# The residual's load and norm put ahead of the memory's in the setup of a two-layer decoder step

## The reference, cut to what matters

```
D_MODEL = 1024
def rms_norm(x, gain):
    x32 = x.astype(jnp.float32)
    y = x32 * lax.rsqrt(jnp.mean(x32 * x32, axis=-1, keepdims=True) + EPS)
    return (y * gain.astype(jnp.float32)).astype(x.dtype)
...
def mem_kv(mem, gain, w_kv, k_gain):
    B, M, _ = mem.shape
    m = rms_norm(mem, gain) @ w_kv
    k = rms_norm(m[..., :MEM_WIDTH].reshape(B, M, MEM_HEADS, MEM_HEAD_DIM), k_gain)
    v = m[..., MEM_WIDTH:].reshape(B, M, MEM_HEADS, MEM_HEAD_DIM)
    return k, v
...
    for i in range(DEPTH):
        hp = rms_norm(xp, norm_mix[i])
        hs = rms_norm(xs, norm_mix[i])
        mkp, mvp = mem_kv(mem_prompt, norm_mem[i], w_mem_kv[i], mem_k_norm[i])
```

## Time and profile before

| what | value |
|---|---|
| median of 3 runs | 3214.2 us (3213.38 to 3219.34) |
| the profiled execution's own time | 3221.07 us |
| its span, first to last instruction | 3219.5 us |
| PE busy in the span | 2985.7 us (93%) |
| DVE, ACT, POOL busy | 1720.0, 1066.8, 93.3 us |
| mean granted TensorE clock | 0.965 of full |

### The profile page before, as it was taken

How to read it: one execution, slowest core, us unless ns; L and a number is a source line. 1 busy time by engine, 2 the same in 40 slices (tenths; PEclk the granted TensorE clock), 3 DMA queues, 4 the chain that set the end, 5 groups by cost and what they waited for, 6 DMA issues and landing times.

```text
span 3219.5 us, 56294 instructions
## 1 busy us (share of the span) xinstructions
PE 2985.7 (93%) x22600; PEld 2691.1 (84%) x22600; DVE 1720.0 (53%) x2527; ACT 1066.8 (33%) x1809; POOL 93.3 (3%) x161
## 2 busy tenths in 40 slices
PE   6996799999999999899975888888999999999997
PEld 6995699999999999799964656556999999999996
DVE  4116224666666666630132666666236666666666
ACT  5223314222222222422233666666032222222221
POOL 0010000000000000000000000000000000000000
PEclk8998899999999999899987999999999999999998
DMA  3122111111111111222316656656301111111101
GB/s 134 51 97 79 64 40 33 40 39 44 54 39 39 39 40 58 81 80 81 101 47 218 229 207 217 206 199 217 110 27 40 43 55 39 39 39 42 56 26 67
DMA packets 190524, 270.05 MB, mean 84 GB/s; under 512 B 9672, under 2 KB 138334, under 8 KB 190396
## 3 DMA queue, kind: packets, MB, share of 16 engines
q1 hardware_dynamic: 171984, 201.68, 18.9%
q0 software_dynamic: 17632, 66.17, 6.3%
q10 hardware_dynamic: 780, 0.34, 0.0%
HBM read 242.70 MB, written 32.14 MB: 85 GB/s over the span
## 4 chain that ended last, share of the span: by engine, by line
PE 82%; DVE 8%; ACT 5%; DMA 2%; issue 1%; ACTq 0%; SPq 0%; POOL 0%; DVEq 0%; POOLq 0%
PE ps L329 23%; PE ps L330 23%; PE ps L331 23%; PE ps L438 2%; PE ps L1146 2%; DVE left L1404 2%; PE ps L1074 1%; DVE x L1953 1%; PE ps L1172 1%; ACT bp_s L1284 1%; PE ps L1086 1%; PE ps L1118 1%; PE ps L1154 1%; DVE bp_s L1406 1%; DMA pk_raw<-in_cache_sb_k_dram 1%
## 5 line engine op out<-in xcount | busy, mean ns | idle before, releaser
L329 PE MATMUL ps<-act_hi,w_hi 128*128 128x370 f32 x2112 | 702.3, 333 | 1.4 <-DVE act_lo L473 1.4
L1953 DVE TENSOR_TENSOR x<-x,ps 128x512 f32<-128x512 f32 (+1 forms) x792 | 538.9, 687 | 305.6 <-PE ps L331 304.7
L330 PE MATMUL ps<-act_lo,w_hi 128*128 128x370 f32 x2112 | 701.6, 332 | 0.0
L331 PE MATMUL ps<-act_hi,w_lo 128*128 128x370 f32 x2112 | 699.7, 331 | 0.0
L329 PE MATMUL ps<-w_hi,act_hi 128*128 128x256 f32 (+1 forms) x1800 | 507.0, 282 | 5.9 <-DVE w_lo L325 1.8
L330 PE MATMUL ps<-w_lo,act_hi 128*128 128x256 f32 (+1 forms) x1800 | 506.3, 281 | 0.0
L331 PE MATMUL ps<-w_hi,act_lo 128*128 128x256 f32 (+1 forms) x1800 | 504.8, 280 | 0.0
L329 PEld LDWEIGHTS ps<-act_hi,w_hi 128*128 128x128 f32 x2112 | 398.7, 189 | 5.7 <-DVE act_lo L473 1.7
L330 PEld LDWEIGHTS ps<-act_lo,w_hi 128*128 128x128 f32 x2112 | 398.4, 189 | 2.0
L331 PEld LDWEIGHTS ps<-act_hi,w_lo 128*128 128x128 f32 x2112 | 398.0, 188 | 0.0
L325 DVE TENSOR_TENSOR w_lo<-w_raw,w_hi 128x2048 fp32r<-128x2048 f32 x73 | 167.3, 2292 | 350.7 <-ACT w_hi L321 350.7
(11 more groups left out here) (285 smaller groups left out, 3568.6 us busy)
## 6 DMA issues: line engine op xcount, KB each, us to landing
pk_raw<-in_cache_sb_k_dram SPq DMA_DIRECT2D x128, 384.0 KB, 3.7
w_raw<-in_w_up_dram SPq DMA_DIRECT2D x88, 512.0 KB, 4.7
d_raw<-in_w_down_dram POOLq DMA_DIRECT2D x44, 512.0 KB, 3.8
projected<-stage POOLq DMA_DIRECT2D x13, 1024.0 KB, 5.2
pv_hi<-in_cache_sb_v_dram SPq DMA_DIRECT2D x32, 384.0 KB, 4.2
pv_lo<-in_cache_sb_v_dram SPq DMA_DIRECT2D x32, 384.0 KB, 4.1
pv_raw<-in_cache_sb_v_dram SPq DMA_DIRECT2D x32, 384.0 KB, 4.3
pv_own<-in_cache_sb_v_dram SPq DMA_DIRECT2D x32, 384.0 KB, 4.4
```

Of the source, the lines that this page charges most:

```text
L329: pe.matmul(out, ahi, bhi, start=first, stop=False, **kw)
L330: pe.matmul(out, ahi, blo, start=False, stop=False, **kw)
L331: return pe.matmul(out, alo, bhi, start=False, stop=last, **kw)
L1953: dve.tensor_tensor(xs, xs, ps[0:ROWS[t], DN_BANK[(2 * t + c) % 4], :], ALU.add).then_inc(dn_ev, 1)
```

## The change

Four of the engine programs are reordered. SP issues x's three transfers first, without the wait on the nine small loads, and the memory's load after them. ScalarE, VectorE and TensorE do the norm of x first, then the memory's norm, and ScalarE and VectorE make the parts of unit 0 after that. In layer 1 the order of the calls on each engine stays as it was. No instruction is added or removed but for the wait.

```
         def _(sp):
-            load_mem(sp)
-
-            sp.wait_ge(set_ld, 16 * 9)
             for g in range(2):
                 sp.dma_start(x[:, 4 * g:4 * g + 4, :], ...).then_inc(x_ld[g], 16)
             sp.dma_start(x[0:NS, NPT, :], ...).then_inc(x_ld[2], 16)
+            load_mem(sp)
...
             for l in (0, 1):
+                act_norm_x(act, c, 8 * l, False, lambda e, t: x_ready(e, t, l, False))
+                act_mem(act, c, l)
                 if l == 0:
-                    act_mem(act, c, l)
                     split_hi(act, 0, 0)
-                act_norm_x(act, c, 8 * l, False, lambda e, t: x_ready(e, t, l, False))
-                if l:
-                    act_mem(act, c, l)
                 act_kv(act, c, l)
...
             for l in (0, 1):
-                if l == 0:
-                    dve_mem(dve, c, l)
-                    split_lo(dve, 0, 0)
                 dve_norm_x(dve, c, 8 * l, False)
                 if l:
                     dve_tails(dve, 0)
-                    dve_mem(dve, c, l)
+                dve_mem(dve, c, l)
+                if l == 0:
+                    split_lo(dve, 0, 0)
                 dve_kv(dve, c, l)
...
-                if l == 0:
-                    pe_mem(pe, c, l)
-                else:
+                if l:
                     pe.wait_ge(dn_ev, DC + 18 * NFT)
                 pe_norm_x(pe, c)
                 if l:
                     pe_tails(pe, 0)
-                    pe_mem(pe, c, l)
+                pe_mem(pe, c, l)
                 pe_kv(pe, c, l)
```

## The result

The changed kernel took 3227.05 us in the median (3216.54 to 3233.56, 16 runs), the kernel before beside it 3213.79 (3208.13 to 3223.39, 16 runs): a ratio of 1.0035 (95% interval 1.0025 to 1.0046), by which it is 11 us slower (the two medians alone differ by 13.3). Two repetitions gave 1.0029 (1.0017 to 1.0041) and 1.0025 (1.0012 to 1.0038), so 8 to 11 us. Executions more than 1.5% above the fastest of the same kernel are left out of all ratios and, where that is said, of medians. The forecast was +5.0 us, with a range up to 3224.0: the direction was right, the size was not.

A forecast was written before the change was run, and what follows sets the result against it. TensorE was taken to bound the kernel from the input projection on, the weight chain to set its start; +4.1 for the weight chain and +0.9 for the clock gave +5.0 us, 3214.2 to 3219.2 us, range 3213.5 to 3224.0.

The forecast's parts named there:

- The weight chain: Weight units' issue, landing, high and low part, 9.19 us a turn; unit 1 ready at 63.64 against 59.58, 4.1 later.
- x's landing: At the kernel's start, x's first transfer was to land at 9.94 us, with bounds of 9.04 and 11.5.
- the table loads: Two ScalarE table loads of 1.28 us each, formerly under the memory's norm, were to lie on the setup's path.
- the memory's norm: In the setup after the norm of x, no longer under x's loads, it was to add 10.28 us.
- The rival of the drain: Each ScalarE table load in the setup drains the engine first: +7.4 us, 3221.6 in total; chance 0.03.
- The norm of x: In the setup, ScalarE was said to pace it, so it kept its old 27.44 us.
- the small loads may land as late as 18.1 and cost nothing: Setup slack: ScalarE's turns of x begin at 24, less 5.9 us taken from the memory's first turn.
- if the setup products wait past 18: Sign of being wrong: TensorE's setup products, which wait for the small loads, wait past 18 us.
- The starving rival: Small loads in the setup land only near 23, beside SP's 6.5 MB stream: +9.9 us, 3224.1; chance 0.07.
- The clock at the projection: TensorE may start the input projection at its low level: 0 to 1.9 us, taken as 0.9.
- the rival of the clock: Low clock past 6 us at the projection's start costs over 2.3 us; at 8 us, +7.5, 3221.7; chance 0.06.
- a later start there is a later end of the same size: From the input projection's first product on, the end follows TensorE, busy for 2985.7 of 3219.5 us.

The follow-up runs named there:

- e3: Changed kernel with weight unit 0 split ahead of the memory's norm: 3215.05 us, ratio 0.9993 to the kernel before; cut behind the input projection, 266.5 us.
- e2: The changed kernel run a second time, nothing edited: 3227.02 us, ratio 1.0029 to the kernel before.
- e18: The changed kernel run a third time, nothing edited: 3224.06 us, ratio 1.0025 to the kernel before.
- the cut kernels: Both kernels ended behind layer 0's input projection, later work left out: before 268.23 us, changed 275.34 and, on another chip, 272.99 us.
- the pair cut at 500 us: Both kernels ended behind layer 0's output projection, later work left out: before 499.18 us, changed 507.33 us in the medians of all six executions.

## Why the prediction was wrong

**The weight chain: right.** One more turn of the weight chain on the path decides. Its turns took 62.22 - 52.96 = 9.26 and 71.56 - 62.22 = 9.34 us against 9.19, and e3 takes the loss back by moving one step off it.

**x's landing, the table loads, the memory's norm: right within 0.6 us.** x landed at 9.38, 9.30 and 9.56 for 9.94, and the memory's norm took 51.13 - 41.31 = 9.82 for 10.28 (10.42 in e2). The accumulator read ends at 15.55, the load begins at 15.56 and the root at 16.86, so the drain that the Trainium skill, "ScalarE: Activation LUTs", section "What ACT_TABLE_LOAD costs", adds isn't there in this trace either. The rival of the drain falls.

**The norm of x: the step that failed.** It stood in the sum at the old 27.44 us. From x's landing and both table loads to the memory's squares it took 41.31 - 9.38 - 2.56 = 29.37, 31.17 in e2 and 29.02 in e18: 1.6 to 3.7 us more. Two sentences led there. "From 27.91 to 55.35 ScalarE paces the norm of x" is a misreading: from 40.97 to 51.97 TensorE paced it, with four turns made ahead under the squares, so the 27.44 held only with that head start. And "the small loads may land as late as 18.1 and cost nothing": they landed at 18.6 to 18.9, just past that line, as the prediction's own sign of being wrong has it ("if the setup products wait past 18"). The line itself was drawn with the memory's first turn; x's turns take twice the products, and four of them at TensorE's low level, 15 products in 3 us, last 6.4 us. An estimate from these rows: with 21.78 - 18.83 = 2.95 us from landing to first turn, the loads would have to land by about 24 - 6.4 - 2.95 = 14.65 for the old head start. The starving rival had the right mechanism and got 0.07, because the mean of the earlier trace rows hid how little the small loads moved while the memory's load ran.

**The clock at the projection: between its bounds.** 0.9 was taken from 0 to 1.9. The first profile paid nothing (fourth tile 9.27 us after unit 2 is ready, as before), e2 8.02 - 7.43 = 0.6, and e18 6.72 - 4.82 = 1.9 (the fifth tile's delay less that of unit 2, which is ready at 73.89 + 2.30 = 76.19 in e2 and at 73.58 in e18, against 68.76). In e18 TensorE stays low from 73.62 to about 79.7, the 6 us at which the rival of the clock began.

**The sum.** The setup costs 4.8 to 7.1 us in the medians of the cut kernels instead of 5.0, so the norm of x alone would have left the time inside the range. The whole kernels differ by 8 to 11, and what is left over, some 1 to 6 us, took it out. The prediction had nothing there, since "a later start there is a later end of the same size"; whether that sentence fails stays open. One by one the lower ends of the three intervals, 8.0, 5.5 and 3.9 us, leave room for hardly any remainder, but weighted by their widths the three give 9.7 us (7.5 to 11.9, an estimate). The plain delay of 7.3 us cost 6.8 (3 to 11), the pair cut at 500 us tells nothing, and where the rest arises was not found. So the norm of x is the one step shown to have failed, and it explains only a part of the miss; the cause of the rest stays open. e3 has no such remainder (1.7 us under before when cut, some 2 as a whole), so what it shares with the changed kernel, the order of the loads and the late turns of x, is not the likely source, though its interval (6 us under to 2 over) leaves some room. The range also took some 2 us for a median's spread from three runs; sixteen runs of one kernel spread over 15 to 17 us.

## What to carry to other kernels

Before a wait is taken out of a load queue, ask who shares the DMA engines with what it held back: here a queue of small packets, while a stream of large ones ran in full, moved at most about a packet for a packet, thus few bytes, and held up an engine that had been early. When a step moves out from under a load, look one link further, at the buffer that it frees: here the first weight unit's split, moved behind a norm, took away the time in which the second unit had been loading. A stretch in which TensorE runs at its low level is free only while another engine covers it, and a stage's old duration is carried over only with the head start that it had.

## What the runs showed of the hardware

0.34 MB in 780 small packets took until 18.6 to 18.9 us beside SP's stream in three executions of the changed kernel and until 8.65 beside 1 MB of it; from 9 to 14 us they got 0.16 MB in 357 packets to SP's 1.61 MB in 394. The granted clock's row isn't to be trusted ahead of the first change in an execution: it says 1.00 at 22 to 25 us while the products run at the pace of 0.50. And at which moment TensorE's level rises within the same work differs between executions by some 3 us (products at the high pace from about 25 us in the first profile and 28 in e2), and with it the end of x's norm moved by 1.7 us.
